# A recurrence's factor 1 - a^2 as tanh(z)(1 + a^2), the square on ScalarE, in place of a reciprocal on VectorE

## The reference

```
u = dwconv(rx) + conv_b
r = sigmoid(u @ wa + ba)        # per block of 128 channels, per direction
i = sigmoid(u @ wx + bx)
log_a = -8 * softplus(-lam) * r
a = exp(log_a)
b = sqrt(-expm1(2 * log_a)) * (i * u)      # sqrt(1 - a^2) * i * u
h = scan over the tokens of  h = a * h + b
```

## Time and profile before

| | |
|---|---|
| median of three runs | 2974.34 us (2973.43 to 2976.2) |
| profiled execution | 2977.02 us, span 2975.2 us |
| busy in the span | PE 88%, DVE 48%, ACT 31%, GpSimd 23% |
| granted TensorE clock, mean | 0.952 |
| chain that ended last | PE 62%, DMA 14%, DVE 14%, ACT 7% |
| L675, reciprocal of 128x512, x12 | 3353 ns each, 91.0 to 190.2 us |
| L677, product, x12 | 692 ns each |
| L642, L647, tanh and exp of 128x256, x24 each | some 500 ns each |
| L654, square root of 128x512, x12 | 630 ns each |
| ACT_TABLE_LOAD | 1283 ns each |

### The profile page before, as it was taken

One profiled execution on the slowest core, in us unless ns is written; L12 is line 12 of the kernel. 1 busy time (PEld: TensorE's weight loads), 2 busy tenths in 40 slices (PEclk: granted clock), 3 DMA queues, 4 the chain that ended last, 5 costly groups with the idle time before them and its releaser, 6 DMA issues.

```text
span 2975.2 us, 30360 instructions
## 1 busy us (share of the span) xinstructions
PE 2632.1 (88%) x11408; PEld 1776.3 (60%) x11408; DVE 1430.9 (48%) x3191; ACT 918.6 (31%) x2319; POOL 678.2 (23%) x615
## 2 busy tenths in 40 slices
PE   7777999879999999999897899999799999887776
PEld 6665888756884878765453566565376655443222
DVE  3775333251001233474656564545755554676444
ACT  2452111210000220244523244532334442333333
POOL 0010111110000000133343222333322333433332
PEclk9888999989999999998999998999899999999999
DMA  6220211114333677999899998999999899998997
GB/s 252 85 81 35 81 62 43 71 57 156 142 145 116 249 262 285 387 421 352 321 382 405 354 393 336 419 412 419 392 360 390 334 385 418 401 374 333 421 421 329
DMA packets 109986, 839.09 MB, mean 282 GB/s; under 512 B 12176, under 2 KB 12432, under 8 KB 13968
## 3 DMA queue, kind: packets, MB, share of 16 engines
q0 software_dynamic: 73728, 536.90, 45.0%
q1 hardware_dynamic: 36112, 300.25, 25.7%
HBM read 836.06 MB, written 1.05 MB: 281 GB/s over the span
## 4 chain that ended last, share of the span: by engine, by line
PE 62%; DMA 14%; DVE 14%; ACT 7%; issue 2%; POOL 1%; SPq 0%; DVEq 0%; POOLq 0%; ACTq 0%
PE psm L2143 17%; DMA mem<-in_puv,mem 13%; PE psm L430 10%; PE psm L1713 6%; PE psm L438 5%; DVE mem L2187 3%; PE psm L719 3%; PE psm L1351 3%; PE psm L2018 3%; PE psm L1248 3%; PE psm L1905 2%; PE psm L1399 1%; DVE mem L675 1%; PE psm L434 1%; PE psm L734 1%
## 5 line engine op out<-in xcount | busy, mean ns | idle before, releaser
L2143 PE MATMUL psm<-mem 128*128 128x512 f32 x2048 | 1027.8, 631 | 156.0 <-ACT mem L2161 150.1
L2171 POOL DMA_INDIRECT mem<-in_puv,mem x512 | 562.0, 1098 | 1218.3 <-PE psm L2143 1149.7
L2187 DVE CUSTOM_DVE_ANT_0 mem<-mem 128x1024 f32<-128x1024 f32 x512 | 624.6, 1224 | 432.0 <-DMA mem<-in_puv,mem 431.4
L2143 PEld LDWEIGHTS psm<-mem 128*128 128x128 f32 x2048 | 375.8, 197 | 612.9 <-issue 302.1
L430 PE MATMUL psm<-mem 128*128 128x256 f32 (+2 forms) x1504 | 353.5, 398 | 55.2 <-DVE mem L537 36.4
L430 PEld LDWEIGHTS psm<-mem 128*128 128x128 f32 x1504 | 293.7, 198 | 114.2 <-issue 53.2
L2155 ACT ACTIVATE mem<-mem 128x1 f32<-128x1 f32 x512 | 102.5, 200 | 685.7 <-DVE mem L2187 684.7
L1713 PE MATMUL psm<-mem 128*128 128x256 f32 x1024 | 239.4, 385 | 0.5 <-ACT mem L1427 0.5
L1713 PEld LDWEIGHTS psm<-mem 128*128 128x128 f32 x1024 | 196.8, 193 | 56.8 <-issue 31.6
L2161 ACT ACTIVATE mem<-mem 128x128 f32<-128x128 f32 x512 | 206.0, 402 | 17.6 <-PE psm L2143 1.0
L438 PE MATMUL psm<-mem 128*128 128x128 f32 x1408 | 190.3, 279 | 19.4 <-ACT mem L987 5.9
(11 more groups left out here) (356 smaller groups left out, 2419.0 us busy)
## 6 DMA issues: line engine op xcount, KB each, us to landing
mem<-in_w2g SPq DMA_DIRECT2D x64, 1024.0 KB
mem<-in_w SPq DMA_DIRECT2D x18, 2048.0 KB, 8.4
mem<-in_pwq SPq DMA_DIRECT2D x32, 1024.0 KB
mem<-in_w2f SPq DMA_DIRECT2D x28, 1024.0 KB
mem<-in_wgu SPq DMA_DIRECT2D x11, 2048.0 KB, 7.5
mem<-in_w2t SPq DMA_DIRECT2D x20, 1024.0 KB
mem<-in_w2b SPq DMA_DIRECT2D x16, 1024.0 KB
mem<-in_w2o SPq DMA_DIRECT2D x16, 1024.0 KB
```

The costliest lines, as they stand in the source:

```text
L2143: m = pe.matmul(bank(6 + h), DG[:, n % 4, :], GR[n % PING][:, 1024 + h * 512:1536 + h * 512], start=k == 0, stop=k == 127)
L2171: po.indirect_dma_start(GR[n % PING], None, A[f"puv{i // 2}"], bass.IndirectOffsetOnAxis(ap=IX[i % 2][:, k:k + 1], axis=0)).then_inc(gsem[ ...
L2187: ve.tensor_tensor_reduce(out=GR[n % PING][:, 0:1024], in0=GR[n % PING][:, 0:1024], in1=X[:, i % 2, :], scale=1.0, scalar=0.0, op0=MUL, op ...
```

## The change

With a = exp(-z), tanh(z) = (1 - a^2) / (1 + a^2). So 1 - a^2 is tanh(z) (1 + a^2). ACT gets one more instruction for each block, the square of a into the scratch tile TF, behind the exp and with a wait for it; DVE's three instructions become one, (TF + 1) * RB. The wait for the scratch tile (`RV["q", b - 2]`) moves from DVE to ACT. A mark "s2" is added for ACT. Nothing else is altered.

```
-                                                     + [(n, b) for b in js for n in ("th", "ex")]
+                                                     + [(n, b) for b in js for n in ("th", "ex", "s2")]
...
                     e.then_inc(RAc.next(("ex", b)), 1)
+                    ac.wait_ge(*RAc["ex", b])
+                    if b >= 2:
+                        ac.wait_ge(*RV["q", b - 2])
+                    ac.activation(TF[:, j % 2, :], RA[:, j, :], ACT.Square).then_inc(RAc.next(("s2", b)), 1)
                     yield
...
                     T_ = TF[:, j % 2, :]
-                    if b >= 2:
-                        ve.wait_ge(*RV["q", b - 2])
-                    ve.wait_ge(*RAc["th", b])
-                    ve.tensor_scalar(T_, RB[:, j, :], 1.0, None, ADD).then_inc(ov.up(), 1)
-                    ve.wait_ge(*ov.now())
-                    ve.reciprocal(T_, T_).then_inc(ov.up(), 1)
-                    ve.wait_ge(*ov.now())
-                    ve.scalar_tensor_tensor(RB[:, j, :], RB[:, j, :], 2.0, T_, MUL, MUL).then_inc(RV.next(("q", b)), 1)
+                    ve.wait_ge(*RAc["s2", b])
+                    ve.scalar_tensor_tensor(RB[:, j, :], T_, 1.0, RB[:, j, :], ADD, MUL).then_inc(RV.next(("q", b)), 1)
                     yield
```

## The result

The changed kernel takes 2946.88 us (median of five runs, 2939.67 to 2950.45), the kernel before 2973.43 (five runs, 2968.19 to 2976.2). The ratio is 0.991, with a 95% interval of 0.9897 to 0.9923: faster by 26.5 us, 0.9%. The profiled execution took 2943.86 us, its span is 2942.0 us.

A forecast was written before the change was run, and what follows sets the result against it. DVE was taken to pace the first half, with PE waiting for its convolutions. The two halves' 26.1 us plus 1.1 at the seam made 27.2, taking the median 2974.3 to 2947.1; range 2940 to 2955.

The forecast's parts named there:

- What comes to ACT: ACT's queue in the recurrence: twelve Squares of 0.63 us, raising its period per block from 1.74 to 2.40 us.
- rival 2: ACT's switch to Sqrt also empties its pipeline, costing another 1.30 us each time: gain 24.6, time 2949.7; chance 3%.
- rival 4: Square does not share the table: two loads, 2.6 us, per block, so 2976 and no measurable difference; chance 2%.
- The new first half: First six recurrence blocks: conv 2 done at 102.2, scans from 106.5 instead of 119.58, pair 6 at 124.4; gain 13.1 us.
- rival 1: All of DVE's 46 us of removed work are gained, ACT's chain hiding everywhere: 2928; chance 2%.
- The second half: Blocks 6 to 11: paced by PE up to its pair 9, then the first half's figures repeat, another 13.1 us.
- The seam: Passage to the delta stage: DVE's copy of the last small projection decides, sigmoid at 191.85; total gain becomes 27.2 us.
- PE's waits: PE's waits for DVE's convolution L537 sink from 36.4 to some 19 us: 1.2, 4.0 and 4.2 in either half.
- Behind it: From the delta stage to the end: the whole shift of 27.2 us is carried, weight loads and expert fetches moving too.
- rival 3: Part is given back by a later transfer that does not move with the work: half the gain, 2961; chance 4%.
- Rival 5: Slower: expert fetches lose pace through different rounding and timing against weight loads; at 10% longer waits 2990; chance 2%.

The follow-up runs named there:

- e1: The kernel before, with an unread Square of a added on ACT for each block and the reciprocal kept on DVE: 2966.99 us, ratio 0.9991.
- e2: The changed kernel without its Squares, DVE multiplying tanh(z) by (1 + tanh(z)), so another factor is computed: 2935.53 us, ratio 0.9888.
- e3: The changed kernel with each Square made twice, the first into a spare tile: 2946.33 us, ratio 0.9925.
- e4: The changed kernel with the square of a made by DVE instead of ACT, same result: 2940.62 us, ratio 0.9897.
- e5: The changed kernel run again unaltered: 2941.10 us, ratio 0.9916 against the kernel before.
- e6: The changed kernel with DVE's last two scans of each half moved behind the next convolution: 2941.63 us, ratio 0.991.
- e8: The kernel of e7 with five of the six Silus moved to where ACT idles ahead of its conv 11: 2929.39 us, ratio 0.9879.
- e7: The changed kernel with the square made on DVE and the scans spread as in e6: 2929.95 us, ratio 0.9871.

## Why the prediction was right

The forecast of 2947.1 stands against 2946.88, the forecast gain of 27.2 against 26.5 between the medians and 26.1 in the stage, and the stage lets each step be checked.

- *What comes to ACT.* Period 2.40 forecast and measured; the Square 0.63, taken from the Sqrt of the same size. The table load costs 1.30, so rival 2 (3%) is out, and no load stands between exp and tanh, so rival 4 is out.
- *The new first half.* Conv 2 done at 102.2, measured 100.76 + 2.43 - 0.96 = 102.2. Scans at 106.5, measured 106.6. Pair 6 at 124.4, measured 124.5. e1 shows that removing the reciprocals, and not the new form as such, is what gives: with them in place, the Squares change nothing. e2 and e3 show the other bound: ACT's chain, not DVE's own work, decides how much of the 46 us comes through. That is why rival 1 fails. What I had not seen is that PE's clock stands behind this chain: where the chain is shortened (e2, e4), a slow half pair takes part of the gain.
- *The second half.* 13.1 forecast again; the last scans moved from 209.50 to 184.51 - 0.96 = 183.55, 25.95 in place of 26.1.
- *The seam.* This is the step with an error. I let pair 11 take 7.0 us, DVE's copy decide, and the sigmoid come at 191.85. Pair 11 took 8.67, ACT's Silus ended at 192.58 and the table load decided: 192.93 with the origin taken off, 26.1 us earlier than before and not 27.2. In e5 it was 9.78 and another 1.1 was gone. The bound that I had written beside it (9.46, gain 25.6) covers the first, but not e5, whose gain is 25.0. That TensorE's clock decides nothing, as I wrote, was so in the first half. At the seam it was not: pair 11 ran at a granted clock of 0.82 (175.9 to 184.6 us), and ACT's conv 11 and its Silus came later for it.
- *PE's waits* were forecast at 19 and are 15.4. I had put 4.2 before pair 6; it is 2.4, since pair 5 ran slower and filled the rest. The start of pair 6 is not touched by that.
- *Behind it* the shift is carried in full, 972.4 us in place of 972.5 to the first expert product. The ratios in the table leave nothing to be given back later either, so rival 3 is out.
- *Rival 5*, slower fetches: from first to last start the expert stage took 1763.5 us before and 1762.5 in e1, with the old arithmetic. With the new it took 1755.6 and 1752.9 in the changed kernel's two profiles, 1762.5 in e3, and 1752.7 to 1758.6 in e4 and e6 to e8. It was never slower with the new form, so the rival is out. Whether it is a little faster these profiles alone do not show, since those of before and e1 are of executions 4 and 9 us above their medians. The medians speak against it: they gain 26.5 us where the stage gains 26.1. In the profiled executions most of the scatter lies in this stage, 11 us from end to end. Its cause was not sought.

That the median lands within 0.2 us of the forecast is luck beyond the mechanism. The stage gained 1.1 less than forecast; the two further runs of the kernel before brought its median 0.9 below the one that I counted from, and the scatter gave the rest back.

## What to carry to other kernels

When a slow instruction leaves the engine that paces a stage, add up the next engine's queue step by step before counting the gain: here 46 us of DVE work became 26 us of time, because ACT's chain of six blocks and a table load had to end before the first scan. A cheap new operation belongs on the engine that waits at that place, and long uninterrupted work should be broken up so that the instruction which releases TensorE comes first; both together were worth some 13 us more than the change alone. The order has to be looked at again where the stage ends: in e7 and e8 it makes the last convolution wait for two blocks of scans. Where whole runs scatter by 10 us, a stretch between two events of the trace tells effects of 2 us apart; for smaller ones it has to be profiled more than once.

## What was not expected

A shorter stage moved TensorE's low clock onto the path. In the changed kernel PE paused 1.27 us before pair 4 and 3.85 before pair 5, and pair 5 then ran at a granted 0.81 where it had time to spare. In e4, PE worked through pair 4 without a pause, paused 1.59 before pair 5, which ran at full pace, and 3.98 before pair 6, whose first half then ran at 0.55 and lasted 6.52 us instead of 3.69. So 3.8 us won ahead of pair 6 shrank to 1. Not every pause of that size did it: in e3 pair 4 came 3.35 us after pair 3 and ran 32 records in 7.14 us. The length of the slow stretch also differs between executions of one kernel: pair 11 took 8.67 and 9.78.
